# A two-layer mixer and mixture-of-experts trunk: the last four chunks of the value projection raw for both token blocks, and weight units issued in another order

## The reference

```python
def hybrid_mixer(h, w_in, w_out, ...):
    p = h @ w_in                                   # 1024 -> 2560 columns
    q, k = rotary(p[..., 0:512]), rotary(p[..., 512:1024])      # 8 heads x 64
    y_att = moba_attention(q, k, p[..., 1024:1536])             # v
    y_sg = spatial_gating(gelu(p[..., 1536:1792]), gelu(p[..., 1792:2048]), ...)
    y_cv = conv_module(p[..., 2048:2304], p[..., 2304:2560], ...)   # GLU, 31 taps, norm, swish
    return concatenate([y_att, y_sg, y_cv]) @ w_out
def grouped_moe(h, ...):                           # 16 experts, 512 wide, two of them per token
    for e in range(16):
        out += gates[:, e] * ((silu(h @ w_gate[e]) * (h @ w_up[e])) @ w_down[e])
for l in range(2):
    h = layer_norm(ALPHA * h + hybrid_mixer(h, ...))
    h = layer_norm(ALPHA * h + grouped_moe(h, ...))
```

## Time and profile before

| | us |
|---|---|
| median of 3 runs | 641.16 |
| range of the runs | 640.29 to 641.18 |
| the profiled execution | 642.03 |
| its span | 640.3 |

### The profile page before, as it was taken

One profiled execution on the slowest core, in us unless ns is written; L12 is line 12 of the kernel. 1 busy time (PEld: TensorE's weight loads), 2 busy tenths in 40 slices (PEclk: granted clock), 3 DMA queues, 4 the chain that ended last, 5 costly groups with the idle time before them and its releaser, 6 DMA issues.

```text
span 640.3 us, 8170 instructions
## 1 busy us (share of the span) xinstructions
PE 618.4 (97%) x3239; PEld 335.2 (52%) x3239; DVE 298.5 (47%) x619; ACT 208.1 (33%) x465; POOL 148.7 (23%) x139
## 2 busy tenths in 40 slices
PE   9999999999999999997999999999999999999993
PEld 5887887534344344342488878764344344344331
DVE  6898897122141231230578988851141231330326
ACT  5831963232032131130184368342032131131211
POOL 1999400440000000000049971007000000000000
PEclk9999999999999999999999999999999999999998
DMA  8999299999999999999999646999999999999991
GB/s 358 431 425 415 108 427 360 377 430 427 412 426 428 427 426 427 427 425 429 429 428 381 234 198 272 416 338 416 432 417 426 431 423 428 427 425 423 432 383 69
DMA packets 21785, 246.70 MB, mean 385 GB/s; under 512 B 3276, under 2 KB 3404, under 8 KB 6384
## 3 DMA queue, kind: packets, MB, share of 16 engines
q1 hardware_dynamic: 18576, 236.56, 88.5%
q10 hardware_dynamic: 1152, 5.77, 2.3%
q0 software_dynamic: 2016, 3.82, 1.6%
HBM read 246.51 MB, written 3.15 MB: 390 GB/s over the span
## 4 chain that ended last, share of the span: by engine, by line
PE 80%; DMA 11%; DVE 7%; issue 1%; ACT 1%; DVEq 0%
PE bank L765 28%; PE bank L790 15%; PE bank L651 13%; DMA ring<-in_units 11%; PE bank L816 4%; PE bank L625 4%; PE bank L871 2%; DVE w_split L1470 2%; PE bank L883 2%; PE bank L731 2%; PE bank L698 1%; PE bank L639 1%; PE bank L777 1%; PE bank L953 1%; PE bank L579 1%
## 5 line engine op out<-in xcount | busy, mean ns | idle before, releaser
L765 PE MATMUL bank<-ring,xe_pair 128*64 128x512 f32 x976 | 213.3, 593 | 5.7 <-DMA ring<-in_units 5.7
L765 PEld LDWEIGHTS bank<-ring,xe_pair 128*64 128x64 f32 x976 | 71.3, 137 | 145.0 <-issue 134.0
L790 PE MATMUL bank<-ring,area_b 128*64 128x512 f32 x480 | 107.0, 596 | 1.6 <-DVE area_b L1693 1.6
L1691 DVE TENSOR_TENSOR area_b<-area_b,bank 128x512 f32<-128x512 f32 x16 | 11.0, 688 | 205.9 <-PE bank L765 205.9
L1326 POOL DMA_INDIRECT rows<-normal_rows,tiny_i x14 | 14.4, 1026 | 267.6 <-DVE tiny_i L1643 240.4
L1310 POOL TENSOR_TENSOR in_lo<-ring,in_hi 128x512 fp32r<-128x512 f32 x56 | 72.0, 1334 | 12.2 <-ACT in_hi L1081 12.2
L1158 ACT ACTIVATE area_b<-bank 128x512 f32<-128x512 f32 x16 | 9.6, 597 | 187.3 <-PE bank L765 187.3
L790 PEld LDWEIGHTS bank<-ring,area_b 128*64 128x64 f32 x480 | 32.9, 137 | 66.9 <-issue 59.0
L1136 ACT ACTIVATE xe_pair<-bank,small 128x128 f32<-128x128 f32 x128 | 47.0, 466 | 45.9 <-PE bank L731 35.6
L1277 POOL TENSOR_TENSOR rstd<-var_eps,tiny 128x1 f32<-128x1 f32 x18 | 10.6, 594 | 191.8 <-DVE var_eps L1402 191.8
L1712 DVE SCALAR_TENSOR_TENSOR y_lo<-bank,tiny,y_hi 128x512 fp32r<-128x512 f32 x32 | 24.0, 750 | 59.7 <-ACT y_hi L1171 59.7
(11 more groups left out here) (206 smaller groups left out, 789.4 us busy)
## 6 DMA issues: line engine op xcount, KB each, us to landing
ring<-in_units SPq DMA_DIRECT2D x101, 2048.0 KB, 19.5
ring<-in_units SPq DMA_DIRECT2D x8, 1024.0 KB, 23.0
ln_par<-in_ln_rows ACTq DMA_DIRECT2D x4, 1024.0 KB, 10.5
extra<-in_units SPq DMA_DIRECT2D x2, 2048.0 KB, 13.8
extra<-in_units SPq DMA_DIRECT2D x2, 1536.0 KB, 19.9
expert_half<-in_units SPq DMA_DIRECT2D x2, 1024.0 KB, 8.6
normal_rows<-mix SPq DMA_DIRECT2D x4, 512.0 KB, 8.8
h<-in_x SPq DMA_DIRECT2D x2, 512.0 KB, 4.1
```

The lines of the kernel that those rows point to most:

```text
L765: mm = pe.matmul(bank[2 + m][e * SLOTS:(e + 1) * SLOTS, :], x[:, k, at + e * SLOTS:at + (e + 1) * SLOTS], w[c][:, m, e, :], start=k == 0, ...
L790: mm = pe.matmul(bank[5 + n][e * SLOTS:(e + 1) * SLOTS, :], hidT[:, k, e * SLOTS:(e + 1) * SLOTS], w[:, k, e, :], start=k == 0, stop=k == ...
```

## The change

Three things change.

- Chunks 28 to 31 of the input projection are raw for both token blocks. The pieces `late_hi` and `late_lo`, ScalarE's and GpSimd's work for them, and their waits go. `IN_CHUNKS`, the number of split chunks per layer, is 28 instead of 32.
- `LOAD_ORDER` begins 0, 2, 3, 4, 5, 1 instead of 0, 3, 4, 5, 1, 2. Unit k=2 waits for the first slab only, and k=1 for the last split chunk of block 1 instead of for the whole late half.
- The rest of extra 0 and extra 1 are issued ahead of `expert_half` and the saving of rows, and wait only for the output projection.

```diff
-LOAD_ORDER = (0, 3, 4, 5, 1, 2) + tuple(range(6, PAIR_UNITS * PAIRS))
+LOAD_ORDER = (0, 2, 3, 4, 5, 1) + tuple(range(6, PAIR_UNITS * PAIRS))
...
-IN_CHUNKS = 4 * KC
-LATE = 3 * KC + KC // 2
+IN_CHUNKS = 3 * KC + KC // 2
...
                 for k in LOAD_ORDER:
                     src = units[l, SLABS + k]
                     if k == EXTRAS[0]:
+                        sp.wait_ge(chunk_used, 2 * KC * (l + 1))
+                        sp.dma_start(extra[0][:, EARLY:], src[:, EARLY:]).then_inc(extra_landed[0], 16)
+                        continue
+                    if k == EXTRAS[1]:
+                        sp.dma_start(extra[1][:, :], src).then_inc(extra_landed[1], 16)
                         sp.wait_ge(norm_ready, TB * (l + 1))
                         sp.wait_ge(strips_pe, TB * (l + 1))
                         sp.dma_start(expert_half[:, :], units[l, SLABS, :, 0:HALF]).then_inc(first_half_landed, 16)
                         for b in range(TB):
                             sp.dma_start(normal_rows[l][b * P:(b + 1) * P, :], normal[:, b, :]).then_inc(normal_saved, 16)
-                        sp.wait_ge(chunk_used, 2 * KC * (l + 1))
-                        sp.dma_start(extra[0][:, EARLY:], src[:, EARLY:]).then_inc(extra_landed[0], 16)
-                        continue
-                    if k == EXTRAS[1]:
-                        sp.dma_start(extra[1][:, :], src).then_inc(extra_landed[1], 16)
                         continue
                     n = ring_unit(l, k)
-                    if k in (1, 2):
-                        sp.wait_ge(used, l * LAYER_UNITS + 5)
+                    if k == 1:
+                        sp.wait_ge(in_chunk_used, IN_CHUNKS * (l + 1))
                     elif n >= RING:
                         sp.wait_ge(used, used_by(n - RING))
...
-                if i >= LATE and b == 0:
+                if i >= IN_CHUNKS:
                     mm = pe.matmul(dst[:, :], xT[:, c, b * P:(b + 1) * P],
                                    unit_at(l * RING_UNITS + 1 + n)[:, c * BANK:(c + 1) * BANK],
                                    start=c == 0, stop=c == KC - 1)
...
-                    if b == 0 or i >= LATE:
+                    if b == 0:
                         pe.wait_ge(in_lo_ready, IN_CHUNKS * l + i + 1)
...
-                        if b == TB - 1 and k == 1:
+                        if b == TB - 1 and k == 1 + (i == IN_CHUNKS - 1):
                             mm.then_inc(in_chunk_used, 1)
...
-                for i in range(LATE, IN_CHUNKS):
-                    in_w_low(l, i)
```

More of the change, by code:

```diff
@@ L284, in trunk @@
                 (area_a_at, (0, 1, 2, 3, 5)), (area_b_at, (1, 2, 3)), (uv_at + 8192, range(4)), (uv_at, range(2)),
-                (uv_at + 4096, range(2)), (ln_par_at, range(4)), (xT_at, range(4)), (area_b_at + 8192, range(2))))
+                (uv_at + 4096, range(2)), (ln_par_at, range(4)), (xT_at, range(2)), (area_b_at + 8192, range(2))))
         in_m = [mix_at + 2048]
         in_hi_at = (in_a + in_b + in_u + in_m + in_v + in_a[:1] + in_ln + in_a[4:] + in_c + in_m +
-                    in_x[:2] + in_h + in_x[2:] + in_c)
+                    in_x + in_h)
         in_hi = [nc.alloc_sbuf_tensor_at(f"in_hi{i}", [P, BANK], F32R, offset=at) for i, at in enumerate(in_hi_at)]
@@ L292, in trunk @@
         in_lo = {at: nc.alloc_sbuf_tensor_at(f"in_lo{at}", [P, UNIT], F32R, offset=ring_at + 4 * UNIT * at) for at in in_slots}
-        late_hi, late_lo = ([[nc.alloc_sbuf_tensor_at(f"late_{name}{l}_{i}", [P, BANK], F32R,
-                                                      offset=ring_at + 4 * UNIT * (l * RING_UNITS % RING) + at + 4 * BANK * i)
-                              for i in range(4 * KC - LATE)] for l in range(DEPTH)] for name, at in (("hi", 0), ("lo", 2 * UNIT)))
         xe = nc.alloc_sbuf_tensor_at("xe", [P, KC, GROUP * P], F32, offset=xT_at)
@@ L452, in used_by @@
             return l * LAYER_UNITS + u + len(EXTRAS) * (u >= SLABS + EXTRAS[0]) + 1
-        def in_high(l, i):
-            return in_hi[i] if i < LATE else late_hi[l][i - LATE]
         def in_low(l, i):
-            if i >= LATE:
-                return late_lo[l][i - LATE][:, :]
             return in_lo[(l * RING_UNITS + 1 + i // KC) % RING][:, i % KC * BANK:(i % KC + 1) * BANK]
@@ L645, in in_product @@
                         pe.wait_ge(xi_lo_ready, TB * l + b + 1)
-                    if b == 0 or i >= LATE:
+                    if b == 0:
                         pe.wait_ge(in_lo_ready, IN_CHUNKS * l + i + 1)
-                    w_hi = in_high(l, i)[:, :]
+                    w_hi = in_hi[i][:, :]
                     w_lo = in_low(l, i)
@@ L1075, in in_w_high @@
                     act.wait_ge(landed[n % RING], 16 * (n // RING + 1))
-                if in_after[i] and i < LATE:
+                if in_after[i]:
                     act.wait_ge(in_chunk_used, IN_CHUNKS * l + in_after[i])
@@ L1080, in in_w_high @@
                     act.wait_ge(xi_lo_ready, TB * (l + 1))
-                act.activation(in_high(l, i)[:, :], unit_at(n)[:, i % KC * BANK:(i % KC + 1) * BANK], ACT.Copy)\
+                act.activation(in_hi[i][:, :], unit_at(n)[:, i % KC * BANK:(i % KC + 1) * BANK], ACT.Copy)\
                    .then_inc(in_hi_ready, 1)
@@ L1309, in in_w_low @@
                 at, cols = (l * RING_UNITS + 1 + i // KC) % RING, slice(i % KC * BANK, (i % KC + 1) * BANK)
-                pool.tensor_tensor(in_low(l, i), ring[:, at, cols], in_high(l, i)[:, :].bitcast(F32),
+                pool.tensor_tensor(in_low(l, i), ring[:, at, cols], in_hi[i][:, :].bitcast(F32),
                                   ALU.subtract).then_inc(in_lo_ready, 1)
@@ L1335, in _ @@
                     router_weights(0)
-                for i in range(min(LATE, 4 * KC - 2)):
+                for i in range(IN_CHUNKS):
                     in_w_low(l, i)
                 rotate(l, 0)
-                for i in range(4 * KC - 2, LATE):
-                    in_w_low(l, i)
                 rotate(l, 1)
```

## The result

The changed kernel takes 649.71 us (median of 7 runs, 645.65 to 652.13) against 640.84 us for the kernel before in the same comparison (7 runs, 639.57 to 643.35): a ratio of 1.0141, interval 1.0118 to 1.0165. The prediction had slower as the likeliest sign, but +1.4 us and a range that ended at 645.6; it is +8.9 us. In the profiled executions the span is 648.0 us against 640.3, +7.7: that of the changed kernel took 649.71 us, its median, and that of before 642.03 us, 1.2 above its median.

The account below looks back on a forecast made before the run. TensorE bounds the kernel nearly everywhere, with the DMA queue in charge at each layer's last weight units. Pairs starting 0.9 us later, less 0.2 given back, in both layers sum to +1.4 us: 642.6 us, range 638.8 to 645.6.

Parts of the forecast that it names:

- The raw chunks: Token block 1, chunks 28 to 31: raw matmuls cost TensorE +0.70 us per layer, reaching the start of the pairs.
- Slot 0 sooner: Queue before the pairs: units k=1 and k=2 load earlier, but the 4.9 and 2.7 us gained turn into idle time.
- Unit 8: Weight load before the pairs: issued at 100.95, lands between 108.8 and 111.1, taken as 109.5 us in layer 0.
- behind 1.75 units of queue: Start of the pairs: expert_half waits for unit 8 and the extras, so the pairs start 0.9 us later per layer.
- the queue dry behind it: After the extras and saved rows: queue idle from some 118.5 us until gate unit 0 frees slot 7.
- The release that was at 165.39: Second pair, layer 0: TensorE's freeing of a slot sets the queue's place to the layer's end; 0.9 us later.
- the rival with the lead carried to the end (C): Ends of both layers: the queue keeps the early unit's lead, -2.1 us, 639.1 us in all; chance 0.15.
- Rival B: Start of the pairs: expert_half is in time, delay 0 to 0.2 us, 641.0 us in all; chance 0.13.
- the size of the landing: Start of the pairs: expert_half lands at 118.1 in layer 0, priced at 4.9 us per unit behind unit 8.
- Rival A: Start of the pairs: expert_half shares the rings with the saved rows, lands at 120.5; +6.2 us, 647.4 us; chance 0.12.
- its sign of a first pair after 120: Start of the pairs, layer 0: a first pair after 120 us would show expert_half sharing the rings, a 3.3 us delay.
- what is given back: End of each layer: remaining DMA backlog absorbs part of the later start, taken as 0.2 us per layer.

Follow-up runs that it names:

- raw_only: Kernel before with only chunks 28 to 31 raw for both token blocks; old load order and old place of the extras: 642.01 us, ratio 1.0022.
- eh_first: Changed kernel with expert_half and the saved rows issued ahead of the extras again; raw chunks and sooner slot 0 stay: 642.12 us, ratio 1.0011.
- before_held: Kernel before with 18 matmuls of constants ahead of the first expert products, delaying TensorE alone: 647.65 us, ratio 1.0103.
- extras_later: Kernel before with the two extra places given to later-read units k=21 and 22, loaded behind k=8: 640.35 us, ratio 0.9992.
- after_again: The changed kernel itself, timed once more against the kernel before: 650.90 us, ratio 1.0147.
- after_busy: Changed kernel with 12 matmuls of constants behind the gather of the first pair's tokens, where TensorE would idle: 648.25 us, ratio 1.0121.
- after_busy_5: Same kernel as after_busy, compared again beside after_again: 647.51 us, ratio 1.0099.
- extras_only: Kernel before with only the extras' new place, both issued ahead of expert_half: 647.98 us, ratio 1.0113.
- eh_rest_rows: Kernel before with the rest of extra 0 issued between expert_half and the saved rows: 640.50 us, ratio 0.9993.
- the second comparison: The changed kernel timed again against the kernel before, as after_again: 650.90 us, ratio 1.0147.
- rest_ahead: Changed kernel with only the rest of extra 0 ahead of expert_half, extra 1 behind the saved rows: 643.65 us, ratio 1.0047.
- later_rest_rows: Kernel before with the edits of both extras_later and eh_rest_rows: 640.14 us, ratio 0.9994.

## Why the prediction was wrong

**Right, by its own steps.** The raw chunks: 70.01 to 76.19 is 6.18 us where 5.47 stood, +0.70 as worked out; raw_only measures +1.1 us for both layers, of the 1.4 that 0.70 twice would be. Slot 0 sooner is worth nothing, because the queue runs dry before the w_out slabs free the next places: 15 GB/s in 88 to 92 us, and eh_first equals raw_only within 0.1 us. Unit 8, predicted to land at 109.5, was issued at 100.80 and landed 8.8 us later, at 109.6. SyncE's timeline of the changed kernel (start us, us), for this issue, for the two extras and for the release below:

```profile
100.80 0.33 SPq L504 DMA_DIRECT2D ring<-in_units  x1
...
105.37 0.33 SPq L486 DMA_DIRECT2D extra<-in_units  x1
105.74 0.43 SPq L489 DMA_DIRECT2D extra<-in_units  x1
...
169.46 0.33 SPq L504 DMA_DIRECT2D ring<-in_units  x1
```

And the DMA views of the same stretches, which end with the us to landing (the extras are told apart by their size):

```profile
ring<-in_units SPq DMA_DIRECT2D x1, 2048.0 KB, 8.8
...
extra<-in_units SPq DMA_DIRECT2D x1, 2048.0 KB, 11.7
extra<-in_units SPq DMA_DIRECT2D x1, 512.0 KB, 6.6
...
ring<-in_units SPq DMA_DIRECT2D x1, 2048.0 KB, 8.4
```

That `expert_half` would open the expert loop behind 1.75 units of queue was right, and so was the queue dry behind it, 48 GB/s in 120 to 124 us. The release that was at 165.39 is 4.07 us later, its unit landing 8.4 us after (7.5 to 8.5 was predicted). With before_held this shows that a later start is a later end, which refutes the rival with the lead carried to the end (C): the last gate unit comes 184.7 and 184.5 us after the start of the pairs, not a microsecond nearer than the 184.2 and 183.0 of before. That it is this one release that sets the end, as the prediction had it, the runs don't bear out: extras_later took away the gap ahead of it and gained nothing that can be measured. Rival B, no delay, needed a landing before 117.3; it came at 119.9.

**First step that failed: the size of the landing.** The step "109.5 + 1.75 x 4.9 = 118.1" has the right order, and in this execution the right landing of unit 8, but prices what follows at a full queue, 2.1 MB per 4.9 us. From unit 8's landing to `expert_half`'s it was 8.6 us by that price and 10.3 in the trace (109.6 to 119.9); in layer 1 it was 10.5. The landings in between say where: the rest of extra 0 at 112.0, 2.4 us behind unit 8 where its quarter unit was priced at 1.2; extra 1 at 117.4, 5.4 behind that for 4.9; `expert_half` 2.5 behind that, as priced. The rates say the same: 299 GB/s in 106 to 109 us and 393 in 109 to 118, against the 426 of the earlier trace rows, which makes 3 x (1 - 299/426) = 0.9 us and 9 x (1 - 393/426) = 0.7 us. A delay of 0.9 us per layer became 2.6 and 3.05, outside the bounds of 0 to 2.4.

The total is firmer than its parts. In layer 0 of three more executions of this order (after_again, after_busy, after_busy_5) unit 8 landed at 110.8 to 111.2, later than the 109.5 taken, and `expert_half` 9.1 to 9.5 us behind it, at 119.9 to 120.6. Nor is it the idle stretch ahead of unit 8 that makes the wait: extras_only keeps the old order of loads, moved 404 GB/s in the same 106 to 109 us, and still took 9.2 us from unit 8 (110.2) to `expert_half` (119.4). What the step lacked is 1.8 to 2.5 us between a landing at the full rate and the landings that were measured; why the queue falls short of that rate is open.

Rival A named the nearest time, 647.4, and its sign of a first pair after 120 was missed by 0.03 us in this execution (119.97) and met in after_again (120.69). Its reason was another one, that the half unit and the saved rows share the rings and are through together. In the profile the rows landed at 120.2 and 122.5, behind `expert_half`, and the 1.7 us between 10.3 and 8.6 had been lost by the landing of extra 1. Still, the rows were issued at 109.57, and no kernel with the extras ahead was run without rows right behind `expert_half`; in the old order eh_rest_rows puts them at about 1 us (5.2 and 5.7 against 6.0 to 6.8 us, and 8.6 in before). A part of A's cause thus isn't ruled out.

**Second step that failed: a term that wasn't in the sum.** TensorE's idle time was priced as idle time. In this kernel the clock can fall to 1.2 GHz at an idle TensorE of about 3 us, and then the first gate stage costs 1.45 to 1.7 us more. In the profile that is 3.15 us, in the medians 1.5 to 3.4 us. No row of before could show it: its waits there are 0.85 and 0.70, and its clock is at full level.

**Third: what is given back.** 0.2 per layer was taken. It was 0.95 in layer 0 and 0.2 in layer 1, and 0.7 and none in before_held. Layer 0 gives back just over the upper bound that the working had for it (0.9), layer 1 the 0.2 that was taken, where up to 2.4 had been allowed.

**The sum, redone with what was measured**: start +2.63 and +3.05, clock +1.43 and +1.70, given back 0.95 and 0.2: +7.7 us, the difference of the spans. The medians differ by 8.9, since the profiled execution of before lies 1.2 us above its median, and by 9.7 in the second comparison.

**Open.** Why the queue moved 299 and 393 GB/s there isn't settled. `expert_half`'s landing in kernels whose SyncE order is the same as before varied between 6.2 (before_held), 6.6 (raw_only) and 8.6 us (before), and in the two layers of rest_ahead between 6.4 and 9.1; nothing here explains it. Nor is it settled what decides whether and when the clock falls.

## What to carry to other kernels

An urgent transfer issued behind prefetches waits for them (10.4 to 11.4 us to landing here, where it had taken 5.1 to 8.6), so a prefetch whose reader is far off belongs behind it; and a landing worked out at the full rate came 1.8 to 2.5 us too early, so give it a margin. Price a wait of TensorE of about 3 us twice, once for the wait and once for what the clock may lose behind it; where it can't be removed, matmuls of constants take the second price away. Where a freed place decides when a load may start, as here, loads moved ahead of that place gained nothing, and a start that was later was later at the end. And look where the profiled execution lies among the runs before its times are taken for those of the kernel.

## What the runs showed of the hardware

The granted clock after an idle TensorE isn't decided by the wait alone. Ahead of the first pair, in the profiled executions, waits up to 1.65 us left the stage at 13.88 to 13.96 us. Of the longer ones, 2.89 gave 15.40; 3.06, 3.40, 3.61 and 3.62 gave 15.65; but 3.15 gave 13.95. Nor does the fall come at one distance from the last matmul: in layer 0 of the changed kernel the granted clock was at half by 119.6 us, 2.5 us into the wait and before TensorE had started again (0.78 in 119.4 to 119.6, 0.50 from there on); in layer 0 of after_again it was still 1.00 at 120.7, when the wait of 3.61 us was over, and 0.50 from 121 on. The changed kernel's runs lie from 645.65 to 652.13, a wider spread than that of before (639.57 to 643.35), and the fall comes in some executions and not in others: the fastest run has a mean granted clock of 0.995, as the kernel before has, and the other six have 0.990 to 0.993. It isn't all of the spread, as the slowest has 0.993. The Trainium skill, TensorE: Matmul & The Clock Gate, section "What's actually happening", has the number of slow matmuls at the start of a kernel differ from run to run, which agrees with that.

The one megabyte of `expert_half` took 5.1 us from issue to landing at best (later_rest_rows) and 11.4 at worst (after_again): the size says little of the landing, the place in the queue much.
